# A decoder layer on one core: the last two expert units finished apart, all other expert rows read back while they run

## The reference

```python
combine = jnp.sum(jax.nn.one_hot(idx, N_EXPERTS) * gates[..., None], axis=1)
for gi in range(N_EXPERT_GROUPS):
    gu = jnp.einsum('td,edf->tef', ht, w_gu[sl])
    g_act, up = jnp.split(gu, 2, axis=-1)
    act = jax.nn.silu(g_act) * up * combine[:, sl, None]
    out = out + jnp.einsum('tef,efd->td', act, w_dn[sl])
```

## Time and profile before

| what | value |
|---|---|
| three runs | 1193.30, 1193.43, 1196.03 us; median 1193.43 |
| the profiled execution's own time | 1192.7 us |
| its span | 1190.9 us |
| mean granted clock of TensorE | 0.982 of full speed |
| busy in the span | PE 94%, PEld 52%, DVE 45%, ACT 30%, POOL 11% |
| bytes moved | 196.35 MB, mean 165 GB/s |
| chain that ended last, by engine | PE 75%, DVE 11%, issue 4%, ACT 3%, DMA 1% |

### The profile page before, as it was taken

The page is one execution under the profiler, slowest core; times in us unless marked ns, Lnnn a source line. Parts: engine busy times, 40 slices in busy tenths (PEclk is TensorE's granted clock), DMA queues, the critical chain, the costliest instruction groups (busy, mean ns, idle before and its releaser), DMA issues.

```text
span 1190.9 us, 16483 instructions
## 1 busy us (share of the span) xinstructions
PE 1116.9 (94%) x6487; PEld 615.0 (52%) x6487; DVE 537.8 (45%) x1196; ACT 351.6 (30%) x676; POOL 131.5 (11%) x154
## 2 busy tenths in 40 slices
PE   6999999999999899897799999999999999997886
PEld 6545744444844689775474444456643333332232
DVE  6876233334399544796572222335532121211116
ACT  4114631111676332204664100265301111100004
POOL 2000012220000000001100000132011111111004
PEclk9999999999999999999899999999999999999998
DMA  8111022131112452420114000462349999999958
GB/s 284 36 58 53 22 74 78 55 98 48 34 59 110 191 146 68 171 101 1 73 70 177 0 1 1 147 255 99 131 170 347 410 397 426 420 423 425 407 195 335
DMA packets 65973, 196.35 MB, mean 165 GB/s; under 512 B 24444, under 2 KB 41056, under 8 KB 55392
## 3 DMA queue, kind: packets, MB, share of 16 engines
q1 hardware_dynamic: 59184, 178.25, 39.4%
q0 software_dynamic: 6656, 16.95, 3.8%
q10 hardware_dynamic: 48, 0.01, 0.0%
HBM read 167.38 MB, written 33.05 MB: 168 GB/s over the span
## 4 chain that ended last, share of the span: by engine, by line
PE 75%; DVE 11%; issue 4%; ACT 3%; DMA 1%; POOL 0%; DVEq 0%; SPq 0%; POOLq 0%; ACTq 0%
PE bank L2643 20%; PE bank L1554 13%; PE bank L1610 8%; PE bank L1577 6%; PE bank L1672 2%; PE bank L1625 2%; PE bank L2770 2%; PE bank L1540 1%; PE bank L805 1%; PE bank L916 1%; PE bank L866 1%; PE bank L1692 1%; PE bank L853 1%; PE bank L884 1%; DVE arena L756 1%
## 5 line engine op out<-in xcount | busy, mean ns | idle before, releaser
L2643 PE MATMUL bank<-arena 128*128 128x512 f32 (+3 forms) x1032 | 357.4, 506 | 6.6 <-ACT arena L2147 5.4
L2643 PEld LDWEIGHTS bank<-arena 128*128 128x128 f32 x1032 | 196.4, 192 | 161.6 <-issue 140.7
L1554 PE MATMUL bank<-arena 128*32 128x512 f32 x1344 | 152.4, 606 | 14.6 <-issue 13.7
L1554 PEld LDWEIGHTS bank<-arena 128*32 128x32 f32 x1344 | 46.4, 112 | 116.7 <-issue 116.7
L1610 PE MATMUL bank<-arena 128*128 128x512 f32 x220 | 95.6, 592 | 0.0
L1327 DVE TENSOR_TENSOR arena<-arena,bank 128x256 f32<-128x256 f32 x21 | 8.9, 422 | 158.3 <-ACT arena L1213 122.6
L1577 PE MATMUL bank<-arena 128*32 128x512 f32 x672 | 76.5, 595 | 2.4 <-ACT arena L1217 1.4
L2147 ACT ACTIVATE arena<-bank 128x512 f32<-128x512 f32 (+1 forms) x57 | 28.5, 505 | 164.4 <-PE bank L2643 163.9
L1370 DVE TENSOR_TENSOR arena<-arena,bank 128x512 f32<-128x512 f32 x32 | 22.0, 689 | 100.1 <-PE bank L1610 79.5
L1610 PEld LDWEIGHTS bank<-arena 128*128 128x128 f32 x220 | 41.3, 190 | 49.7 <-issue 49.7
L1213 ACT ACTIVATE arena<-bank 128x256 f32<-128x256 f32 x21 | 8.1, 384 | 165.7 <-PE bank L1554 165.7
(11 more groups left out here) (411 smaller groups left out, 1585.8 us busy)
## 6 DMA issues: line engine op xcount, KB each, us to landing
arena<-in_w_e_gu SPq DMA_DIRECT2D x26, 2048.0 KB, 14.3
arena<-in_w_e_dn SPq DMA_DIRECT2D x32, 1024.0 KB, 15.0
arena<-in_w_in SPq DMA_DIRECT2D x11, 1024.0 KB, 5.2
arena<-y_d SPq DMA_DIRECT2D x8, 1024.0 KB, 11.1
arena<-hz_d SPq DMA_DIRECT2D x4, 1792.0 KB, 8.9
arena<-in_w_e_gu SPq DMA_DIRECT2D x6, 1024.0 KB, 13.1
arena<-in_w_e_gu SPq DMA_DIRECT2D x12, 512.0 KB, 14.3
pk_d<-arena SPq DMA_DIRECT2D x8, 640.0 KB, 2.9
```

What stands on the lines that cost most here:

```text
L1554: ins = mm(bank[part, :], hgT[:, k, part], w_gu(es[i] % NB, k), start=(k == 0), stop=(k == KT - 1))
L2643: ins = mm(psum[PROJ_BANKS[u % 3]][0:rows, 0:n], lhs(k), rhs(k), start=(k == 0), stop=(k == kt - 1))
```

## The change

Units 19 and 20 (`LATE` = 2) are no longer scattered to `y_d`. Their results stay in the two `ysb` buffers. All tokens are finished in a first set of eight row groups from what the other 19 units scattered, and the tokens that have a pair in units 19 or 20 are finished in two further groups (`NT` and `NT`+1, one per late unit), whose rows overwrite, or take the place of, those of the first set.

- `y_d` is cleared at the start of the program (eight DMAs of 1 MB from a zero tile, behind the weight chunks 4 to 7 of the first projection), so that rows never scattered read as zero.
- `x2` is stored to `x2_d`, 512 KB behind each store of `xn_d`, and the weights of the pairs to `w_d` in elements of 8 bytes. `fin_g` is loaded ahead of the experts.
- While units 3 to 9 run, small operations on DVE, PE and GpSimd find which rows of the late units belong to the same token (`lt_S`), the index of each token's other pair (`ix_ot`), which rows GpSimd's stores are to leave out (`ix_out`), and fetch the late pairs' weights from `w_d` (four indirect DMAs, `late_weights`).
- SyncE reads `y_d` back when the down product of unit 18 is done and the scatters of units 17 and 18 have landed; the `yg` buffers lie where slots 2, 3 and 4 were.
- GpSimd gathers the late tokens' rows of `x2_d` and, when the scatters have landed, of their other pair from `y_d` (`pool_late`).
- The sum of a row group no longer runs on PE: ACT scales y0 by w0 (`first`), GpSimd adds x2, DVE adds w1\*y1 (`sum`); ACT squares (`square`), DVE scales all groups (`scale`). A first piece stands inside the loops of units 20 and 21.
- A late group is x2 + w\*other pair (DVE, `other`) + a product of `lt_S` and `ysb` on PE (four matmuls of 512 columns each).
- Row groups 0 to 4 are stored by SyncE, 5 to 7 and the late ones by indirect DMAs of GpSimd; the first late store waits until those of SyncE have landed.
- The branch of the overflow now stands behind the whole tail, with a tail of its own in its body.

The diff, cut to its core:

```diff
-        yg = [view(i * TK * D, TK, D) for i in range(6)] + [view(o_g2 + i * TK * D, TK, D) for i in range(2)]
-        y_out = [view(o_g1 + i * D, D) for i in range(NT)]
+        yg = [view(o, TK, D) for o in (EW, EW + TK * D, EW + 2 * TK * D, o_g1, o_g1 + TK * D, o_g3,
+                                       o_g1 + 2 * TK * D, o_g1 + 3 * TK * D)]
+        xr = [view(o, D) for o in (o_tmp + 6 * D, o_cx)]
+        yo = hg
...
+                sp.wait_ge(s["t_m_e"], 2 * (m + 1))
+                sp.dma_start(x2_d[m * P:(m + 1) * P, :], x2[:, m]).then_inc(s["t_x2"], 16)
...
-            sp.wait_ge(s["t_r_dve"], 4)
+            sp.wait_ge(s["t_r_dve"], 6)
+            sp.dma_start(w_d.rearrange("(m p k) o -> p m (k o)", p=P, k=TK), w_mk).then_inc(s["t_xn"], 16)
+            sp.wait_ge(s["t_x2"], X2_STORED)
+            sp.dma_start(fin_g, a["norm_final"].unsqueeze(0).to_broadcast([P, D])).then_inc(s["t_x2"], 16)
             sp_experts(sp, moe, 0)
+            sp_rows(sp, 0)
             with overflow(sp):
...
-            sp_tail3(sp)
...
@@ act_experts, between the copy of actT and the copy of y @@
+                    if isinstance(p, int):
+                        for step in ACT_BESIDE.get(u, ()):
+                            act_rows(act, 0, *step)
                     act.wait_ge(q["dn"], UN * p + u)
...
             pe_experts(pe, mm, moe, 0)
+            pe_late(pe, mm)
             with overflow(pe):
...
+        ORDER = ((0, 1, 2, 3, NT, 4, NT + 1, 5, 6, 7), tuple(range(NT)))
+        ACT_BESIDE = {UN - 1: [("first", 0)], UN: [("first", 1), ("square", 0), ("first", 2)]}
+        ACT_AFTER = ([("first", 3), ("square", 1), ("first", 4), ("square", 2), ("first", 5), ("square", 3),
+                      ("square", NT), ("first", 6), ("square", 4), ("square", NT + 1), ("first", 7),
+                      ("square", 5), ("square", 6), ("square", 7)],
...
+        POOL_STEPS = ([("first", i) for i in range(7)] + [("store", NT), ("first", 7), ("store", NT + 1)]
+                      + [("store", i) for i in BY_POOL], [("first", i) for i in range(NT)])
+        DVE_BESIDE = {UN - 1: [("sum", 0), ("sum", 1)]}
+        DVE_AFTER = ([("scale", 0), ("sum", 2), ("other", NT), ("other", NT + 1), ("scale", 1), ("sum", 3),
+                      ("scale", 2), ("sum", NT), ("scale", 3), ("sum", 4), ("scale", NT), ("sum", NT + 1),
+                      ("scale", 4), ("sum", 5), ("scale", NT + 1), ("sum", 6), ("scale", 5), ("sum", 7),
+                      ("scale", 6), ("scale", 7)],
...
@@ act_rows, "first" @@
+                y_wait(act, i, r)
+                nc.scalar.activation(yg[i][:, 0], yg[i][:, 0], ACT.Copy,
+                                     scale=wts[:, 0, i:i + 1]).then_inc(s["t_m_pt"], 1)
...
@@ pool_rows, "first", and the late store @@
+                pool.wait_ge(s["t_m_pt"], 2 * NT + NT * r + i + 1)
+                nc.gpsimd.tensor_tensor(yg[i][:, 0], yg[i][:, 0], x2[:, i], ALU.add).then_inc(s["t_m_dg"], 1)
...
+                if l == 0:
+                    pool.wait_ge(s["l_w"], L_OUT)
+                    pool.wait_ge(s["f_ot"], 16 * (3 + len(BY_SP)))
...
@@ dve_rows: "sum", "other", "scale" @@
+                dve.wait_ge(s["t_m_dg"], NT + NT * r + i + 1)
+                v.scalar_tensor_tensor(yg[i][:, 0], yg[i][:, 1], wts[:, 1, i:i + 1], yg[i][:, 0], ALU.mult,
+                                       ALU.add).then_inc(s["f_c"], 1)
...
+                link(v.scalar_tensor_tensor(xr[l], yo[l], w_ot[:, l:l + 1], xr[l], ALU.mult, ALU.add))
...
+                link(v.reciprocal(rms[:, c], rms[:, c]))
+                v.scalar_tensor_tensor(row_out(i), sum_of(i), rms[:, c], fin_g, ALU.mult,
+                                       ALU.mult).then_inc(s["xs_r"], 1)
...
@@ sp_rows @@
+                if r == 0 and m == 0:
+                    sp.wait_ge(moe["dn"], UN - LATE)
+                    for i in range(2):
+                        sp.wait_ge((moe["st0"], moe["st1"])[(UN - LATE - 1 - i) % 2], rows_of(UN - LATE - 1 - i))
+                if r == 0 and m == 3:
+                    sp.wait_ge(moe["gu"], UN - 1)
+                if r == 0 and m == 6:
+                    sp.wait_ge(moe["dn"], UN - 1)
...
+            for m in BY_SP if r == 0 else range(NT):
+                sp.wait_ge(s["xs_r"], G4 + place_of(r, m) + 1)
+                sp.dma_start(out[m * P:(m + 1) * P, :], yg[m][:, 1]).then_inc(s["f_ot"], 16)
+            sp.wait_ge(s["f_ot"], 16 * (3 + len(BY_SP) + r * NT))
+            sp.wait_ge(s["l_w"], L_OUT + 16 * (LATE + len(BY_POOL)))
...
+                if c >= 4:
+                    clear_rows(2 * (c - 4))
+                    clear_rows(2 * (c - 4) + 1)
+            sp.wait_ge(s["consts_v"], Y_CLEARED)
```

More of the change, by code:

```diff
@@ L1199, in sp_tail @@
                 pass_end(sp, moe, PASSES - 1)
-            sp_tail3(sp)
+                sp_rows(sp, 1)
         def overflow(eng):
@@ L1305, in act_tail2 @@
             act_experts(act, moe, 0)
+            for step in ACT_AFTER[0]:
+                act_rows(act, 0, *step)
             with overflow(act):
@@ L1310, in act_tail2, with dve_experts @@
                     pass_end(act, moe, p + 1)
-            act_tail3(act, link, stats)
-        def dve_experts(dve, v, q, p):
+                for step in ACT_AFTER[1]:
+                    act_rows(act, 1, *step)
+        def dve_experts(dve, v, q, p, link=None):
             def tokens(u):
@@ L1530, in dve_tail2 @@
                     pass_end(dve, moe, p + 1)
-            dve_tail3(dve, v, link, inverse_rms)
+                for step in DVE_AFTER[1]:
+                    dve_rows(dve, v, link, 1, *step)
         def pe_experts(pe, mm, q, p):
@@ L1863, in pool_tail2 @@
             pool_experts(pool, moe, 0, last_row, last_y)
+            pool_late(pool, moe, last_row, last_y)
+            for step in POOL_STEPS[0]:
+                pool_rows(pool, 0, last_row, *step)
             with overflow(pool):
+                pool.wait_ge(s["l_w"], L_OUT + 16 * (LATE + len(BY_POOL)))
+                for u in late_u:
+                    scatter(pool, moe, u, last_y)
                 pass_end(pool, moe, 0)
@@ new lines, in hybrid_trunk @@
+        DVE_BESIDE = {UN - 1: [("sum", 0), ("sum", 1)]}
[3 more added lines that the diff above has]
+                      ("scale", 6), ("scale", 7)],
+                     [("sum", 0)] + [st for i in range(1, NT) for st in (("sum", i), ("scale", i - 1))]
+                     + [("scale", NT - 1)])
@@ new lines, in late_counts, with late_sums @@
+        def late_counts(pe, mm):
+            pe.wait_ge(s["t_m_mx"], NT + 2)
+            for l in range(LATE):
+                for of in range(LATE):
+                    ins = mm(psum[7][:, 8 + l:9 + l], lt_S[:, of, l], ones[:, 0:1], start=(of == 0),
+                             stop=(of == LATE - 1))
+            ins.then_inc(s["t_m_sc"], 1)
+        def late_sums(dve, v, link):
+            dve.wait_ge(s["t_m_sc"], NT + 2)
+            link(v.scalar_tensor_tensor(lt_odd, psum[7][:, 8:8 + LATE], 1.5, lt_odd, ALU.is_gt, ALU.mult))
+            link(v.tensor_scalar(lt_i, lt_odd, float(1 << 20), None, ALU.mult))
+            link(v.tensor_tensor(ix_st, ix_ga[:, late_at], lt_i, ALU.bitwise_xor))
+            dve.wait_ge(s["l_w"], L_W + 32 * LATE)
+            for of in range(LATE):
+                ins = v.tensor_scalar(lt_S[:, of], lt_S[:, of], w_own[:, of:of + 1], None, ALU.mult)
+                ins.then_inc(s["t_m_rc"], 1) if of == LATE - 1 else link(ins)
@@ new lines, in pe_late, with act_rows @@
+        def pe_late(pe, mm):
+            pe.wait_ge(moe["y"], 2 * UN)
+            pe.wait_ge(s["t_m_rc"], NT + 1)
+            for l in range(LATE):
+                for hf in range(2):
+                    for of in range(LATE):
+                        ins = mm(psum[6 * l + hf][:, :], lt_S[:, of, l], ysb[late_u[of] % 2][:, hf * HALF:(hf + 1) * HALF],
+                                 start=(of == 0), stop=(of == LATE - 1))
+                ins.then_inc(s["f_p"], 1)
+        def act_rows(act, r, what, i):
+            if what == "first":
+                y_wait(act, i, r)
+                nc.scalar.activation(yg[i][:, 0], yg[i][:, 0], ACT.Copy,
+                                     scale=wts[:, 0, i:i + 1]).then_inc(s["t_m_pt"], 1)
+                return
+            j = place_of(r, i)
+            c = slice((G4 + j) % 4, (G4 + j) % 4 + 1)
+            act.wait_ge(s["f_c"], j + 1)
+            act.wait_ge(s["xs_r"], G4 + j - 3)
+            nc.scalar.activation(row_sq, sum_of(i), ACT.Square, accum_out=ss[:, c]).then_inc(s["t_q_e"], 1)
+            act.wait_ge(s["t_q_e"], CT * NHALF + j + 1)
+            nc.scalar.activation(rms[:, c], ss[:, c], ACT.Sqrt, bias=epsc[:, 0:1],
+                                 scale=1.0 / D).then_inc(s["rms_r"], 1)
```

240 lines of the change are left out of this document (151 added, 89 removed).

## The result

The changed kernel takes 1206.15 us, the median of four runs (1203.94 to 1208.57), against 1193.37 for the kernel before on the same chip (four runs, 1190.79 to 1196.03). The ratio is 1.0103, with a 95% interval from 1.0078 to 1.0129: it is slower by about 1%. The profiled execution took 1205.52 us, with a span of 1203.7 and a mean granted clock of 0.971.

A forecast was written before the change was run, and what follows sets the result against it. The prediction took full DMA engines to bound the experts and a round trip through memory the tail. VectorE's end, 1179.9 + 10 + 2.5 + 1.9 = 1194.3, plus 4.1 + 0.4 + 3.2 gave span 1202.0, time 1204 us; range 1188 to 1209.

The forecast's parts named there:

- The earlier read-back: Start of the tail: SyncE reads y_d after unit 18's scatter, so y0 is in SBUF at 1144.9, 13.3 us earlier.
- VectorE's list: Tail: VectorE's sums, scalings and other operations total 31.5 us and become what is late, ending at 1179.9 without a stall.
- (a): Tail: GpSimd's additions of x2 hold up VectorE's two-input SBUF operations, taken as 10 us, between 0 and 14.4.
- (b): Head of VectorE's list: row 0 needs its square, a table load and a root, leaving VectorE stalled 2.5 us.
- (c): Near the tail's end: row 7's addition queues behind GpSimd's first late store, which waits for row 4's: 1.9 us.
- The end: Behind VectorE: last row's store by GpSimd 4.1 us, last landing to end 0.4, SyncE's overflow read and jump 3.2.
- Unit 20 stays where it is: Experts: the small operations on VectorE, TensorE and GpSimd, mostly in units 3 to 9, were claimed to cost 0.
- The final gain: Load of the last norm's scale, moved from 1137.57, where it delayed nothing, to a stretch before the experts.
- the first: Rival, tail: GpSimd's additions don't block VectorE's sums, time 1193.8 us, within 0.3% of before; chance 0.16.
- the second: Rival, tail: additions fall into VectorE's waits, with 2 us of stalls and a 1 us jump, time 1189.2; chance 0.18.
- the third's slip: Rival, tail's head: y0 lands late, TensorE's last down product slips with it, all moves by 5 us to 1209; chance 0.11.

The follow-up runs named there:

- e3: The changed kernel with GpSimd's eight additions of x2 to the first eight row groups left out: 1196.86 us, ratio 1.0007 to the kernel before.
- e4: The changed kernel with the eight additions of x2 made by VectorE instead of GpSimd, nothing left out: 1200.02 us, ratio 1.004 to the kernel before.
- e6: The changed kernel without the two late groups' stores, SyncE storing all eight others, its last waits behind the overflow branch: 1202.09 us, ratio 1.0061.
- e2: The changed kernel with SyncE's final waits for the stores behind the overflow branch instead of ahead of it: 1209.07 us, ratio 1.0107.
- e5: The changed kernel with the late rows' small operations on VectorE, TensorE and GpSimd moved to units 15 to 18: 1205.61 us, ratio 1.0089.
- e12: The changed kernel with sums off GpSimd, small operations later, tail reordered, plus weights' store and final-gain load moved behind unit 1's gate product: 1192.18 us, ratio 0.9981.
- e7_full: The changed kernel without GpSimd's additions: groups 0 to 4 summed on VectorE, 5 to 7 on TensorE, copied out by ScalarE: 1196.51 us, ratio 1.0023.

## Why the prediction was right

The forecast was 1204 us against 1206.15 measured, from a sum of +11.1 us in the profiled execution against +12.8. The mechanism was right: the read-back left the path, VectorE's list took its place, and GpSimd's additions stretched it. The closeness of the number is in part luck, as the steps show:

- **The earlier read-back** held. Gaps measured from the gate product of unit 20: the first load issued 6.2 us behind it (forecast 7.7), y0 in SBUF at 13.0 (13.3), VectorE's first sum at 17.0 (16.8).
- **VectorE's list** was sized too high: the forecast took 1.31 us per operation from the earlier trace rows, where the next operation was of another kind. Alone they follow each other at 1.20. Work 29.8 us from the first sum on, against 31.5 for the whole list.
- **(a) Blocking** was right in kind and near in size: 10 forecast, 8.9 measured, in five pieces of 1.7 to 2.0 rather than seven of 1.14 to 2. Of the seven additions, that of row 2 began inside a scaling and was itself stretched, and that of row 7 ran while VectorE stood idle. (The scaling of the earlier trace rows that it rests on ended 1.08 us behind GpSimd's operation, not 1.01; the sum doesn't use it.) e3 and e4 show it by taking the additions away and by moving them: −11.9 and −5.8 us.
- **(b), (c) Idle time**: 4.4 forecast, 5.0 measured. The piece behind the late store was 1.9, as forecast. In the other the sums waited for GpSimd (1.89) more than for the root (1.09), where only the root's 2.5 was forecast. The 1.9 behind the late store is not a loss of its own: e6 took the wait away, and blocking took its place.
- **The end** was near in its number, 8.5 us behind VectorE against 7.7, and incomplete in its reason. The last store landed 4.0 us after its issue (4.1 forecast) and SyncE's read and jump took 3.2 (3.2 forecast). But the store was issued 1.15 us behind VectorE's end, and the sum has nothing for that. And e2 moved the read and the jump away and gained nothing, because GpSimd's drain ended as late. The prediction moved the last store from SyncE's queue to GpSimd's and priced the landing, but never asked what GpSimd itself needs to end. The jump itself was 2.6 us from the compare at 1200.9 to the drain at 1203.5, with the DMA engines quiet but for the one packet of instructions at 1201.9. By the Trainium skill (Runtime: NRT & Kernel Launch, Instruction fetch mechanics) a taken branch out of the fetched window waits for its target to be fetched. The packet and the 2.6 us agree with that; that SyncE waited for this packet no row shows.
- **"Unit 20 stays where it is"** failed. The step that put eight small matmuls "inside units 3 to 9, where DVE stands idle for most of a unit: 0" looked at the wrong engine: DVE is idle there, TensorE is not. It cost 2.2 us over the experts, of which e5 gave back 1.7, and with them came the slower gate product of unit 20, 1.3 us of the tail.
- **The final gain** was moved to a stretch before the experts, and the weights' store put beside it, with no question of what is under way there. In the one profile of the changed kernel it cost nothing, in nine of eleven with the transfers there the stretch was 2 to 3.4 us longer. e12 moved the weights' store and this load together, so which of the two it was stays open, and one profile doesn't rule out chance.

The profiled execution was 1.7 us longer than the sum: +0.7 ahead of the experts, +2.2 in them, +0.2 at the head of VectorE's list, +0.6 of idle time and +0.8 at the end, against 1.7 of work and 1.1 of blocking that were oversized. The opposite signs are why the sum came out close. The rivals fell by the rows: sums at 3.00 rule out the first, a VectorE busy for 27.5 of 30 us the second; the third's slip of TensorE's last down product did occur, but at 0.8 us (0.75 to 1.58 of wait) and not 5, beside the 1.3 of the slower gate product.

For the larger question: the change does take the round trip through memory off the path: y0 is there 13.0 us behind the gate product of unit 20, where it was 26.7. It puts VectorE's list in its place, which was half hidden before. The list is nine operations of 1024 columns longer (three scalings that GpSimd made, and two sums, two "other" products and two scalings for the late groups), and GpSimd slows five of them. With the sums kept off GpSimd, the small products moved and the two transfers moved, the tail is 55.6 us against 59.3, and the kernel is level with the one before or 0.2% faster (interval 0.9966 to 0.9996), not 1% slower.

## What to carry to other kernels

Before work is handed to GpSimd as help for a full VectorE, look in the trace for one pair of their two-input SBUF operations that overlap: if one of them is stretched to nearly the sum of both, the help costs VectorE more than it saves. Small operations are free only on the engine that has gaps in that unit, and small transfers only where nothing is being gathered just in time; choose their place engine by engine. And look at each engine's own end: let one issue the last store that ends at once behind it (here SyncE, whose drain took 0.01 to 0.06 us, where GpSimd's took about 6).

## What was not expected of the hardware

- GpSimd's drain at the end of the program took about 6 us, whether its last work was a store (6.49 in the changed kernel, 5.94 in e12_weights) or an addition (6.32 in e6_spend). In the kernel before it ended at 1188.0, 5.0 behind GpSimd's last operation, hidden behind SyncE's last stores.
- A gather of 128 rows of x2 issued at 1134.37 landed 12.45 us later, beside the experts' last weights; a y load issued at 1140.68 was awaited until 1147.46.
- TensorE's granted clock was 0.61 in 1165 to 1195 us, where it worked 3.7 of 30 us. Its products for the late groups, at 1158.79, ran 9.94 us for 16 rows, nearly 0.62 each, at a clock of 0.70 (1158 to 1168.8 us), against 0.44 each in e7_full (7.13 for 16 at 1154.23, clock 1.00), where the wait ahead of them was 0.81 and not 5.53 us. The length of the wait alone doesn't decide: behind 2.28 us of it the gate product of unit 20 took 7.08 us in the kernel before, behind 2.32 it took 8.77 in e4_dveadd (clock 0.81 in 1140 to 1149 us).
